# Layer 0: attention units between the later in-projection blocks, and modulation sums in halves

## What is computed

```python
mod = silu(c) @ ada_w[i] + ada_b[i]              # 6 x 1024 values
sh1, sc1, g1, sh2, sc2, g2 = split(mod, 6)
h = rms_norm(x, norm1_g[i]) * (1 + sc1) + sh1
q, k, v = split(h @ w_in, 3)                     # layer 0: 8 heads, q and k in two maps of 64, v of 128
p = softmax(q @ k.T / 8 - slope * dist, masked)  # per head and map
a = p[:, :, 0] - lam * p[:, :, 1]                # differential attention
y = subln(a @ v) @ w_out
x = x + g1 * y
h = rms_norm(x, norm2_g[i]) * (1 + sc2) + sh2
x = x + g2 * moe(h)                              # top group, top 2 of 8 experts in it; 32 experts
```

## Time and profile before

| What | Value |
|---|---|
| median of three runs | 1850.01 us |
| the profiled execution, whole | 1846.84 us |
| its span in the trace | 1845.0 us |
| PE busy | 1684.1 us (91%) |
| DVE busy | 490.1 us (27%) |
| mean DMA rate | 317 GB/s |

### The profile page before, as it was taken

One profiled execution on the slowest core, in us unless ns is written; L12 is line 12 of the kernel. 1 busy time (PEld: TensorE's weight loads), 2 busy tenths in 40 slices (PEclk: granted clock), 3 DMA queues, 4 the chain that ended last, 5 costly groups with the idle time before them and its releaser, 6 DMA issues.

```text
span 1845.0 us, 18530 instructions
## 1 busy us (share of the span) xinstructions
PE 1684.1 (91%) x7537; PEld 859.2 (47%) x7537; DVE 490.1 (27%) x935; ACT 444.2 (24%) x939; POOL 158.4 (9%) x236
## 2 busy tenths in 40 slices
PE   6896999888889879999999999999998999989988
PEld 4643543333333334845464344444443356565564
DVE  1357221000000103244241002221220123553362
ACT  2015211111111102015231013333331034343351
POOL 0212010000000010123000010000001000100000
PEclk9999999999999999999989999999998999999999
DMA  9989779999999999987369989999999963413310
GB/s 359 347 337 397 296 277 409 422 419 420 422 421 421 421 413 396 383 338 258 115 244 410 347 323 397 395 405 420 420 419 410 368 231 107 145 50 117 137 46 23
DMA packets 122752, 585.12 MB, mean 317 GB/s; under 512 B 11936, under 2 KB 16872, under 8 KB 99008
## 3 DMA queue, kind: packets, MB, share of 16 engines
q1 hardware_dynamic: 101008, 489.59, 66.3%
q0 software_dynamic: 21536, 88.72, 13.1%
q10 hardware_dynamic: 112, 5.51, 0.8%
HBM read 578.87 MB, written 21.32 MB: 325 GB/s over the span
## 4 chain that ended last, share of the span: by engine, by line
PE 60%; DMA 25%; DVE 6%; ACT 3%; issue 3%; SPq 3%; ACTq 0%; DVEq 0%; POOL 0%
PE psum L2204 57%; DMA ring<-in_expert_w_up 19%; DMA work<-in_ada_w 3%; SPq L1433 1%; PE psum L699 1%; DMA ring<-in_expert_w_gate 1%; SPq L1402 1%; DMA work<-in_ctx 1%; DMA ring<-in_ada_w 1%; DMA work<-in_w_mod 1%; PE psum L2508 1%; DVE small L1057 1%; PE psum L1198 1%; DVE work L1882 1%; DVE work L2099 0%
## 5 line engine op out<-in xcount | busy, mean ns | idle before, releaser
L2204 PE MATMUL psum<-ring,work 128*64 128x512 f32 (+5 forms) x4272 | 1095.4, 575 | 66.8 <-DMA ring<-in_expert_w_up 53.9
L2204 PEld LDWEIGHTS psum<-ring,work 128*64 128x64 f32 (+2 forms) x4272 | 424.3, 152 | 664.5 <-issue 635.0
L2204 PE MATMUL psum<-work 128*128 128x192 f32 (+9 forms) x1048 | 218.2, 371 | 8.1 <-DVE work L2032 2.6
L2204 PEld LDWEIGHTS psum<-work 128*128 128x128 f32 (+3 forms) x1048 | 144.9, 188 | 105.2 <-issue 81.6
L2099 DVE TENSOR_TENSOR work<-work,psum 128x256 f32<-128x256 f32 x64 | 27.0, 421 | 593.2 <-ACT work L1802 593.2
L1802 ACT ACTIVATE work<-psum 128x256 f32<-128x256 f32 x64 | 24.5, 383 | 607.7 <-PE psum L2204 607.7
L2204 PE MATMUL psum<-work,ring 128*128 128x256 f32 x704 | 158.8, 384 | 3.2 <-DMA ring<-in_diff_w_in 1.1
L2204 PEld LDWEIGHTS psum<-work,ring 128*128 128x128 f32 x704 | 133.4, 192 | 29.1 <-issue 8.1
L1669 ACT ACTIVATE work<-psum 128x256 f32<-128x256 f32 (+5 forms) x184 | 79.7, 443 | 224.7 <-PE psum L2508 76.0
L1561 POOL DMA_INDIRECT expert_rows<-work,targets x56 | 55.1, 984 | 806.6 <-DVE work L2125 806.6
L2125 DVE TENSOR_TENSOR work<-psum,rows 128x512 f32<-128x512 f32 x64 | 44.3, 692 | 255.8 <-PE psum L2204 255.7
(11 more groups left out here) (295 smaller groups left out, 956.6 us busy)
## 6 DMA issues: line engine op xcount, KB each, us to landing
ring<-in_expert_w_gate SPq DMA_DIRECT2D x60, 2048.0 KB, 16.5
ring<-in_expert_w_up SPq DMA_DIRECT2D x60, 2048.0 KB, 17.4
ring<-in_expert_w_down SPq DMA_DIRECT2D x57, 2048.0 KB, 14.4
work<-in_ada_w POOLq DMA_DIRECT2D x40, 1024.0 KB, 8.0
ring<-in_w_in SPq DMA_DIRECT2D x12, 2048.0 KB, 10.1
work<-in_w_mod POOLq DMA_DIRECT2D x16, 1024.0 KB, 6.8
ring<-in_sb_w_in SPq DMA_DIRECT2D x6, 2048.0 KB, 24.7
ring<-in_w_out SPq DMA_DIRECT2D x6, 2048.0 KB, 8.0
```

What stands on the lines that cost most here:

```text
L2204: return T.matmul(out_, lhsT, rhs, start=start, stop=stop, skip_group_check=True)
```

## The change

The in-projection of layer 0 is made in another order of columns (v for heads 0 to 3, q and k for heads 0 to 3, v for heads 4 to 7, then q and k of heads 4 to 7), and `head` makes blocks 0 to 4. The other seven blocks are cut in two column halves of eight matmuls each, 14 in all, and put ahead of attention steps 0 to 11 (three at step 8). Through step 12 the attention pipeline is one step shorter (transposes two, products three steps behind, DVE combines ahead of the next scores), and the scores use one pair of banks.

The summed groups are loaded as 16 parts of 1024 columns into six half buffers, in two column halves; a half is summed over partitions as soon as its eight parts are added up. PE has item 0 after block 3, item 1 after step 0, items 8 and 9 after steps 5 and 8, items 16 to 21 after steps 10, 11, 13, 15, 17 and 19, 22 and 23 after the last step, 24 to 27 after the four blocks of the projection. DVE makes all of sum 1 ahead of attention and sum 2 in it, two parts in each of the steps 0 to 7. SP's waits become 12 and 26 half steps for `w_in` slice 4 and `w_out`; its wait ahead of the expert weights is again "group 3 used". In layer 1 the summed items stand behind blocks 4, 6, 8 and 11. Several semaphores are merged, and ACT squares in place in PSUM.

```diff
+    SLICES = (4, 0, 2, 5, 1, 3)
+    BLOCKS = (("v", 0, 0), ("v", 0, 1), ("q", 1, 0), ("q", 1, 1), ("k", 2, 0), ("k", 2, 1), ("v", 3, 0), ("v", 3, 1),
+              ("q", 4, 2), ("k", 5, 2), ("q", 4, 3), ("k", 5, 3))
+    LAST_USE = (1, 3, 5, 7, 10, 11)
+    WOVEN = 12
+    HALVES = [range(k, k + 1) if k < 8 else range(8, 11) if k == 8 else range(k + 2, k + 3) for k in range(WOVEN)]
+    READY = (5, 6, 10, 12)
...
             if l == 0 and n == 4:
-                sp.wait_ge(sem("ada_used"), 5)
+                sp.wait_ge(sem("ada_step"), 12)
             if l == 0 and n == 6:
-                sp.wait_ge(sem("ada_used"), KT * 2 - 3)
+                sp.wait_ge(sem("ada_step"), 2 * (KT * 2 - 3))
...
             if l == 0:
-                sp.wait_ge(sem("ada_used"), KT * 3)
+                sp.wait_ge(sem("ada_used"), used_by(3))
...
+        def half_free(part):
+            g = group_of(part // 2)
+            if g not in SUMMED:
+                pool.wait_ge(sem("ada_used"), used_by(g - 1) + part // 2 % KT + 1)
+            elif part % KT == KT - 1:
+                pool.wait_ge(sem("ada_used"), used_by(g - 1) + part // KT % 2 + 1)
+            else:
+                pool.wait_ge(sem("ada_step"), steps_by(part + 1))
...
+            if g in SUMMED:
+                for part in (2 * i, 2 * i + 1):
+                    if part >= 6:
+                        half_free(part - 6)
...
+                    pool.dma_start(ada_half[:, part % 6, :], src).then_inc(sem(f"ada_in{part % 6}"), 16)
+                return
             if i >= 3:
+                half_free(2 * i - 6)
+                half_free(2 * i - 5)
...
                 for k in range(16 + 2):
+                    if 1 <= k <= WOVEN:
+                        diff_combine(k - 1)
                     if k < 16:
                         diff_scores(k)
+                    if k >= WOVEN + 2:
                         diff_combine(k - 2)
+                    if k == 1:
+                        ada_take(1)
+                    if k < 8:
+                        ada_sum(2, [2 * k, 2 * k + 1])
+                    if k == 9:
+                        ada_take(2)
...
+            for p in range(5):
+                for c in range(2):
+                    woven_half(p, c)
+                if p == 3:
+                    ada_item(0)
...
+        DIFF_ITEMS[0], DIFF_ITEMS[5], DIFF_ITEMS[8] = [1], [KT], [KT + 1]
+        for at_, k in enumerate((10, 11, 13, 15, 17, 19)):
+            DIFF_ITEMS[k] = [2 * KT + at_]
+        PROJ_ITEMS = [24], [25], [26], [27]
 
         def diff_attention():
-            pe.wait_ge(sem("qkv"), 12)
             for k in range(16 + 4):
+                if k < WOVEN:
+                    for hb in HALVES[k]:
+                        woven_half(5 + hb // 2, hb % 2)
                 if k < 16:
...
+                    pe.wait_ge(sem("qkv"), READY[k // 4])
+                    if k:
+                        pe.wait_ge(sem("a_max"), k if k <= WOVEN else k - 1)
```

More of the change, by code:

```diff
@@ L180, in program @@
     ada_in = carve(3, 4 * 512)
+    ada_half = ada_in.rearrange("p i (a n) -> p (i a) n", a=2)
     base = carve.at
@@ L202, in group_of, with in_count, used_by, steps_by @@
         return 1 + i // KT
-    def in_count(i):
-        return 16 * sum(len(runs(group_of(j))) for j in range(i % 3, i + 1, 3))
+    def in_count(part):
+        loads_of = lambda j: 1 if group_of(j // 2) in SUMMED else len(runs(group_of(j // 2))) * (j % 2 == 0)
+        return 16 * sum(loads_of(j) for j in range(part % 6, part + 1, 6))
+    def used_by(g):
+        return sum(2 if j in SUMMED else KT for j in range(1, g + 1))
+    def steps_by(part):
+        g = group_of(part // 2)
+        return 2 * KT * SUMMED.index(g) + part - 2 * KT * (g - 1) + 1
     def line_count(g):
```

224 lines of the change are left out of this document (140 added, 84 removed).

## The result

Over four runs the changed kernel takes 1880.32 us (1874.47 to 1884.44), beside 1849.95 us (1847.73 to 1850.33) for the kernel before on the same chip: ratio 1.0173, 95% interval 1.0156 to 1.0191. Forecast was 1857, and the stated range ended at 1870. The direction was right; the loss is about 30 us instead of 7. The profiled execution took 1881.25 us, with a span of 1879.5, 34.5 us more than that of before.

A forecast was written before the change was run, and what follows sets the result against it. DMA was taken to bound layer 0's experts, so the first expert's shift, 243.9 to 251.0, 7.1 us, passes to the end: 1846.8 becomes 1853.9, with the median 3.2 above it 1857 us; range 1841 to 1870.

The forecast's parts named there:

- Sum 1: Ahead of item 1 in layer 0: first modulation sum ready at 85 us, bounds 80 and 90, PE idle 12.7 us.
- the clock: Behind PE's idle time before item 1: 3 us lost to the lower granted clock.
- the interleaved steps: Attention steps with half blocks woven in, layer 0: from 85 us, scores 12 reached at 151.5 us.
- The tail: From scores 12 to layer 0's projection: projection starts at 175.7 us, 10.2 us earlier, bounds 168 and 185.
- The projection: Layer 0's projection: 28.3 us plus 4.0 for items 24 to 27 plus 1 of waiting, ending at 209.0.
- Behind the projection: From layer 0's projection to the transposes of x: 15 us, mostly item 30's load, transposes at 224.0.
- Rival (3): Layer 0's projection and behind: starved items, first expert at 262, 1859 to 1868 us; chance 0.24 together with another rival.
- From the transposes to the first expert: Router stretch of layer 0: unchanged at 27.0 us, first expert at 251.0, 7.1 us later.
- The experts pass a shift on one for one: Layer 0's DMA-bound experts: same bytes and slots, so the first expert's shift reaches the end in full.
- The rival of a late gate: Expert weights start some 16 us later, so about no gain, 1850 us; chance 0.15 including mixtures near zero.
- A sign of being wrong that I had named: The forecast is wrong if the shift at the first expert is not the shift at the end.
- Layer 1, "0, up to 3": Halves behind blocks 4, 6, 8 and 11: PE arrives after the parts land, cost 0, up to 3 us.

The follow-up runs named there:

- e4: Kernel before, with only items 24 to 27 moved behind the four blocks of layer 0's projection: 1865.45 us, ratio 1.0081 to 1.0115.
- e12: Kernel before, with items 24 to 27 behind the projection's blocks and the DRAM copy issued just ahead of the experts: 1865.87 us.
- e2: Changed kernel, with the DRAM copy issued just before the first expert instead of at the end of attention: 1862.65 us.
- e13: Changed kernel, the DRAM copy at its old place but with rows interleaved so that each packet is 4 KB: 1871.52 us.
- e10: Changed kernel with the edits of e2 and e3, item 30 behind the router's logits and item 31 behind the rank matmuls: 1851.54 us.
- e11: Kernel before, with the DRAM copy just ahead of the experts and item 31 behind the router's rank matmuls: 1854.07 us.
- e15: e10 with the DRAM copy issued by SP right behind the early down parts of the experts: 1850.80 us.
- e16: e11 with the DRAM copy issued by SP behind the early down parts of the experts: 1854.87 us.
- e1: Changed kernel, with SP's wait ahead of the expert weights ending when item 17 is used, no longer at item 23: 1881.06 us.
- e9: Changed kernel with the edits of e2 and e3, item 30 behind the logits, and SP's expert-weight wait at sum 2 used: 1866.44 us.
- e3: Changed kernel, with layer 1's four summed items behind blocks 2, 5, 8 and 11 instead of 4, 6, 8 and 11: 1870.56 us.
- e18: Kernel before, with the DRAM copy in 4 KB packets and nothing else: 1847.88 us.

## Why the prediction was wrong, step by step

- **Sum 1, the clock, the interleaved steps: right.** Sum 1 was done at 83.6 (85), scores 12 began at 151.89 (151.5).
- **The tail: right.** Projection at 177.25 (175.7). Over ten kernels with the interleaved blocks and the late gate it starts at 174.4 to 177.7, mean 176.3; over the five with the old program at 183.3 to 189.2, mean 185.5. Attention gives 9.2 us; 10.2 were forecast. About 3 of them are no gain of the interleaving: with items 24 to 27 moved out and nothing else, e4 and e12 start at 182.35.
- **The projection: short by 2.7.** With item 27 it ended at 213.3, 36.0 us behind its start (33.3 forecast); items 26 and 27 waited 3.6 us, not 1.
- **Behind the projection: the step that failed.** I took items 28 and 29 for "1 us" and only item 30's 12.4 us as a wait, 15 in all, bounds 6.7 and 22. Measured: 25.4, from 213.3 to 238.7, since items 28, 29 and 30 each waited, 6.3, 8.0 and 5.5 us. I had costed item 30's load by the earlier trace rows as if SP's two new parts were all that was ahead of it, and wrote that the first four land in the projection. But these, issued at 174 instead of 156, had moved only 3.65 of their 8.4 MB by 205, beside the copy and its 57 KB packets, and SP's queue had moved 8.4 only near 221, 8 us behind the projection; DMA was full until 237. The prediction's own terms say as much when they are added up: 8.4 MB of the four parts, 5.5 of the copy, 5.2 of items 26 to 30 and 4.2 of the two new parts are 23.3 MB, by its 0.41 MB/us 57 us from 174, that is until 231 (an estimate); item 30 landed at 236.8. I had set 20 + 14 us of DMA beside the 33 us of the projection and drawn no wait from it. e2 takes the copy away and gets 252.0, 1 us from the forecast; e13 keeps the copy, cuts its packets, and has the transposes 13 us earlier, where e2 has 17. e4 has item 30's wait (11.5 us) by the place of the items alone. Rival (3) had this mechanism and place, a projection that ends at 213 with the transposes 22 us behind it; its first expert at 262 was 5.6 us short.
- **From the transposes to the first expert:** 28.9 in place of 27.0; the first transposes and their warming matmuls ran at the lower clock after PE's 20 us of waiting (the first took 1.76 us instead of 1.16). I had left that out. That the clock is all of the 1.9 us is not shown.
- **The experts pass a shift on one for one: right** in the changed kernel (490.5 us, 489.9 before) and, within 1.4 us, in 14 of 18 profiles; the other four need 8 us more, two for a late early part (e10, e11), two for bytes that idle DMA had left (e15, e16). So the reason I gave, "the same bytes and the same slots", is the condition. The rival of a late gate fell twice (e1, e9).
- **A sign of being wrong that I had named came true:** the shift at the first expert was 23.7 us, the shift at the end 34.5.
- **Layer 1, "0, up to 3": wrong, 11.2.** I asked whether the parts land before PE gets to the item. What decides is when PE frees the buffer: a half summed at 769.2 waited for block 4's end at 793.8, and POOL with it. Of the 11.2, 8.8 lie in the in-projection, and e3 takes 6.7 of these back. What is left, 2.1 us, is two more items, below. The other 2.4 are the slow start of attention.
- **Sum of the misses** up to the first expert: 1.6 (projection's start) + 2.7 (in it) + 10.4 (behind it) + 1.9 (clock) = 16.6, from 251.0 to 267.6. The experts add 0.6, and from layer 1's start to the end it is 10.2 (1121.4 us, 1111.2 before; of the 11.2 about 1 comes back behind the projection): 27.4, the profiled execution's 1881.25 against the forecast 1853.9. The medians differ by 23, because the profiled execution of before lay 3.2 us below its median and this one 0.9 above.

The fit for one DMA (the Trainium skill, DMA: Bandwidth & Descriptors, Anatomy of one DMA), 4.4 us for an item, comes near the measured time for item 24, issued at 170.76 with no other queue at work (5.1 us), and for none behind it: 7.3 us for item 25, and 29.0, 26.2, 25.5, 23.2, 22.9 and 17.8 for items 26 to 31.

Once all three queues have work, their packet counts are nearly the same (48, 48 and 41 from 190 to 200 us; 170, 170 and 171 in e13), whatever the packets hold. That is the rule of turns by packets of the Trainium skill (DMA: Bandwidth & Descriptors, Queues, rings and completion order), and e13 bears it out: the bytes of q10 and the waits of PE went with the size of its packets. From 174 to 190 us the counts differ (50, 296, 107); there POOL's queue had a head start, having worked alone until 174. The 2 KB runs of `w_in` (471 packets to 154) stay outside the rule.

## What to carry to other kernels

A step moved off a buffer's last use moves every load behind it, so cost a moved step by the bytes that stand ahead of the load it needs, summed over all queues from the last time DMA was idle, and not by the duration of one load. A large copy in DRAM belongs where no small load is waited for; failing that, its rows can be ordered so that its packets are small. Work that only frees a buffer for the next load should go to the consumer as soon as it is ready. Ahead of a stretch that DMA bounds, count the bytes moved by the time it starts as well as the time itself: idle DMA there comes back as time (e15, e16).

## What the runs showed of the hardware

- Half an item costs PE as much as a whole one. A half (two matmuls of one row, four records) and an item (four, eight records), in the timeline of PE of the changed kernel, from start to the start behind:

```profile
111.83 1.03 PE L2283 MATMUL psum<-work,cst 128*1 128x512 f32 x4
112.79 3.72 PE L2283 MATMUL psum<-work,ring 128*128 128x256 f32 x16
...
144.52 1.04 PE L2283 MATMUL psum<-work,small 128*1 128x512 f32 x8
145.49 3.72 PE L2283 MATMUL psum<-work,ring 128*128 128x256 f32 x16
```

  0.96 and 0.97 us. A block of the projection, eight matmuls of 512 columns, takes 7.06 us or 0.88 each, so the four of an item, which go to different rows of PSUM, must run side by side. Cutting sums in halves costs 0.96 us for each added half, four in this kernel. I had forecast 0.5 for a half.
- A DRAM to DRAM copy of 5.5 MB took 27.5 us in 57 KB packets and 60.1 us in 4 KB packets beside the same two loaded queues. Small packets aren't slow by themselves: in the kernel before, where less stood beside the copy, it took 22.5 us in large ones and 19.9 in small ones (e18).
- After PE's 20 us of waiting with three short items in them, the granted clock stood at 0.50 (225 to 237 us), the lower level of 1.2 GHz, and the first transposes that followed ran at it; over 237 to 245 us it was 0.80.
